# Expert inputs sorted through a buffer in DRAM instead of gathered by one-hot products, in a two-block transformer kernel

## The chip, the cores and the metric

One core of one Trainium2 chip runs the whole program, with all arithmetic in float32. The metric is the device time of one execution in microseconds (us). The kernel before takes 2696.76 us, the median of three runs (2690.66 to 2697.54).

The engines go by their names in the profile: PE multiplies matrices (PEld loads its weights), DVE, ACT and POOL work on vectors, SP only issues DMAs. PSUM (`ps`) is the memory that PE writes. Sixteen DMA engines serve all queues; queue 1 is SP's, queue 10 ACT's, queue 0 POOL's.

## What is computed

Three layers of mixer and experts follow each other over 512 tokens of width 1024. The mixers are a state-space scan beside forgetting attention, a differential attention, and an RWKV-7 time mix. After each one comes a layer norm, a hierarchical mixture of experts, and another layer norm. Only the experts matter here:

```python
def _hier_moe(h, rg_w, rg_b, re_w, re_b, w_gate, w_up, w_down):
    ...
    e_val, e_idx = lax.top_k(jax.nn.softmax(e_logits, axis=-1), TOP_K)     # TOP_K = 2
    ...
    combine = jnp.sum(jax.nn.one_hot(expert_id, N_EXPERTS) * weights[..., None], axis=1)
    for e in range(N_EXPERTS):
        act = jax.nn.silu(hf @ w_gate[e]) * (hf @ w_up[e])                 # hidden width 512
        out = out + combine[:, e:e + 1] * (act @ w_down[e])
```

The first expert layer has 16 experts and the other two have 32. A token goes to two experts, so each layer has 1024 rows of expert input.

## The kernel before

Each token's two rows get a **slot**: the rows of an expert stand together, padded to blocks of `BLK` = 32. `project_and_experts` (L1072) does the output projection, the first norm, the routing and the experts of a layer. A layer has as many blocks as its experts fill: 42, 52 and 52 with this input (146 in all), at least one per expert, and some experts have up to five. The number of blocks is known only on the chip, so every engine runs a loop with a bound read from `table`.

**Inputs of a block.** PE computes them as a product: `gather(n)` (L1254) multiplies a one-hot matrix (which token sits in which of the 32 slots of block n) with all tokens `x_tok`, 16 matmuls into `ps[:, 5]`. DVE makes the one-hot matrix by three small operations (`hot`, L1388), and transposes the result out of PSUM into `xg` (`take_inputs`, L1476), the stationary operand of the gate and up products. `xg` has one buffer. The gather of block g+1 stands in PE's program between the gate/up products of block g and its down product.

**A block on PE** (L1276 to L1294): wait for `xg`; gate and up products, first half, which need the expert's first weight piece; second half, which needs the second piece; the gather of the next block; then the down product, which needs the third piece, and in two halves the transposed hidden values `hT`. ACT applies silu to each half (L1342), DVE multiplies by the up values (L1490) and transposes (L1493) into `hT`.

**Weights.** An expert has three pieces of 2 MB (gate/up half 0, gate/up half 1, down). Three experts are held at a time: two in `ring`, the third in `arena` and `xt_mem`. SP's `follow` (L1161) waits until the last block of expert e has used a piece and then loads the same piece of expert e+3 into its place, in fixed order. Within a queue the loads come one after another.

**Outputs.** DVE copies a block's result into `y_sb` (L1501, two buffers), and ACT stores it to the DRAM buffer `xybuf` by four DMAs of 32 KB (L1325), rows of 1 KB. At the end of the layer POOL gathers each token's two rows from `xybuf` with 8 indirect DMAs (L230). `xybuf` is filled with zeros once, in the first mixer (L482).

**POOL** is otherwise idle during the expert loop. Ahead of it, it loads the gains and offsets of the second norm (L291, L292, and L296, L297).

## Time and profile before

| | us |
|---|---|
| median of three runs | 2696.76 |
| lowest, highest | 2690.66, 2697.54 |
| the profiled execution | 2697.32 |
| its span in the trace | 2695.6 |
| expert loop of the first layer (42 blocks) | 380.7 to 687.4 |
| expert loop of the second layer (52 blocks) | 1063.2 to 1550.7 |
| expert loop of the third layer (52 blocks) | 2190.5 to 2652.0 |

PE is busy for 2343.1 us (87% of the span), DVE for 1000.8 us, ACT for 571.8 us and POOL for 194.1 us. The DMA queues move 616 MB, 575 MB of it on SP's queue.

The profile is of one execution. The busy share of an engine over the whole span says little here, because the three loops have different limits; each has to be read by itself, from the busy share of PE beside that of the DMA engines. A loop's limit may also change inside it, since one expert has one block and the next has five. In rows of the timeline the first column is the start, the second the length, both in us; "[x <-y]" is idle time of the engine ahead of that row and what ended it.

### The profile page before, as it was taken

Reading aid. Unit: us, or ns where it says so; the run is one execution under the profiler, and the core shown is the slowest. Engines: PE = TensorE matmul, PEld = TensorE weight load, DVE = VectorE, ACT = ScalarE, POOL = GpSimd, SP = SyncE. Lnnn points to the kernel's source line nnn. Section 1 sums busy time; section 2 is a strip of 40 time slices with the busy share of each in tenths; the row PEclk is TensorE's granted clock in tenths of the full one; section 3 lists DMA queues with packets and bytes.
Section 4 is the critical chain, followed back from the end, with each engine's and each line's share of the span. In section 5 each row is a group of like instructions: output and inputs, shape, how many; then the busy total and the mean of one; then the engine's idle time right before and its main releaser. Section 6 shows DMA issues by size and latency. Waiting matters only on the chain. (4 is left out here: it accounts for less than half of the span.)

```text
span 2695.6 us, 88071 instructions
## 1 busy us (share of the span) xinstructions
PE 2343.1 (87%) x38568; PEld 1597.3 (59%) x38569; DVE 1000.8 (37%) x2690; ACT 571.8 (21%) x1231; POOL 194.1 (7%) x309
## 2 busy tenths in 40 slices
PE   8997999999999888999757779978889988788972
PEld 4445557777544655777545533458777466566761
DVE  1206353333400854333212254037765443222324
ACT  2035211111300641111101031033433111111111
POOL 1001200000100010000000010012332200000001
PEclk9998999999999999999989889989999999999996
DMA  9202158977421006969999942000001289999995
GB/s 342 112 32 94 49 216 343 409 309 284 164 94 63 32 19 237 403 271 427 429 429 428 426 173 102 0 24 3 3 5 40 106 313 427 429 429 428 413 428 214
DMA packets 83423, 616.42 MB, mean 229 GB/s; under 512 B 19909, under 2 KB 40649, under 8 KB 49242
## 3 DMA queue, kind: packets, MB, share of 16 engines
q1 hardware_dynamic: 45664, 574.98, 51.6%
q10 hardware_dynamic: 31402, 20.06, 2.4%
q0 software_dynamic: 6224, 19.43, 2.3%
q8 instruction: 105, 1.72, 0.3%
q14 instruction: 28, 0.23, 0.0%
HBM read 582.92 MB, written 31.49 MB: 228 GB/s over the span
## 5 line engine op out<-in xcount | busy, mean ns | idle before, releaser
L1282 PE MATMUL ps<-ring,arena 128*32 128x128 f32 x13184 | 411.3, 285 | 104.4 <-DMA ring<-in_experts 71.4
L1282 PEld LDWEIGHTS ps<-ring,arena 128*32 128x32 f32 x13184 | 382.0, 115 | 146.1 <-DMA ring<-in_experts 68.3
L1259 PE MATMUL ps<-x_tok,arena 128*32 128x256 f32 x4768 | 292.2, 384 | 11.0 <-DVE arena L1397 8.3
L1342 ACT ACTIVATE arena<-ps 128x64 f32<-128x64 f32 x292 | 65.5, 224 | 1085.0 <-PE ps L1282 1085.0
L1490 DVE TENSOR_TENSOR arena<-arena,ps 128x64 f32<-128x64 f32 x292 | 64.8, 222 | 615.6 <-ACT arena L1342 615.6
L1282 PE MATMUL ps<-arena 128*32 128x128 f32 x5504 | 171.6, 283 | 48.2 <-DMA arena<-in_experts 39.4
L1259 PEld LDWEIGHTS ps<-x_tok,arena 128*32 128x32 f32 x4768 | 159.8, 112 | 89.4 <-issue 18.9
L1292 PE MATMUL ps<-ring,arena 128*32 128x256 f32 x3296 | 198.2, 379 | 13.0 <-DMA ring<-in_experts 12.9
L1282 PEld LDWEIGHTS ps<-arena 128*32 128x32 f32 x5504 | 158.3, 113 | 67.0 <-DMA arena<-in_experts 45.4
L1232 PE MATMUL ps<-ring,arena 128*128 128x512 f32 x384 | 171.9, 604 | 3.4 <-PEq L2465 1.7
L1292 PEld LDWEIGHTS ps<-ring,arena 128*32 128x32 f32 x3296 | 109.1, 110 | 85.7 <-DMA ring<-in_experts 21.2
L549 PE MATMUL ps<-xt_mem,ring 128*128 128x512 f32 x320 | 137.9, 593 | 0.0
L1232 PEld LDWEIGHTS ps<-ring,arena 128*128 128x128 f32 x384 | 73.0, 194 | 89.8 <-issue 89.5
L1477 DVE STREAM_TRANSPOSE arena<-ps 128x256 f32<-128x256 f32 x149 | 67.1, 450 | 149.2 <-PE ps L1259 149.2
L1779 PE MATMUL ps<-arena,ring 128*128 128x512 f32 x256 | 110.1, 592 | 0.0
L1602 PE MATMUL ps<-xt_mem,ring 128*128 128x512 f32 x256 | 110.0, 592 | 0.0
L549 PEld LDWEIGHTS ps<-xt_mem,ring 128*128 128x128 f32 x320 | 60.6, 190 | 76.5 <-issue 76.4
L1334 ACT ACT_TABLE_LOAD x73 | 93.7, 1283 | 33.1 <-DVE arena L1468 26.4
L1501 DVE COPY arena<-ps 128x256 f32<-128x256 f32 x146 | 62.0, 425 | 94.7 <-PE ps L1292 94.7
L1292 PE MATMUL ps<-xt_mem,arena 128*32 128x256 f32 x1376 | 83.3, 380 | 5.8 <-DMA xt_mem<-in_experts 4.9
L1779 PEld LDWEIGHTS ps<-arena,ring 128*128 128x128 f32 x256 | 48.6, 190 | 61.6 <-issue 61.6
L1602 PEld LDWEIGHTS ps<-xt_mem,ring 128*128 128x128 f32 x256 | 48.6, 190 | 61.2 <-issue 61.2
(449 smaller groups left out, 2938.3 us busy)
## 6 DMA issues: line engine op xcount, KB each, us to landing
ring<-in_experts SPq DMA_DIRECT2D x165, 2048.0 KB, 21.3
arena<-in_experts SPq DMA_DIRECT2D x50, 2048.0 KB, 24.8
xt_mem<-in_experts SPq DMA_DIRECT2D x25, 2048.0 KB, 29.5
ring<-in_mixer_chunks SPq DMA_DIRECT2D x24, 2048.0 KB, 12.8
xybuf<-arena ACTq DMA_DIRECT2D x608, 32.0 KB, 6.8
xybuf<-arena SPq DMA_DIRECT2D x1, 9216.0 KB, 50.9
ring<-gate_rows SPq DMA_DIRECT2D x2, 2048.0 KB, 7.4
rows<-in_ln_g POOLq DMA_DIRECT2D x6, 512.0 KB, 7.5
```

The costliest lines, as they stand in the source:

```text
L549: ins = pe.matmul(bank, w[:, k, j * P:(j + 1) * P], xT[:, k, :], start=(k == 0), stop=(k == NK - 1))
L1232: ins = pe.matmul(ps[:, 2 * j + c, :], mT[:, k, j * P:(j + 1) * P], w[:, k, :], start=(k == 0), stop=(k == NK - 1))
L1259: ins = pe.matmul(ps[to, 5, 0:W], one_hot[:, j, :], x_tok[:, j, q * W:(q + 1) * W], start=(j == 0), stop=(j == NT - 1))
L1282: ins = pe.matmul(ps[at, 2 + half, 0:P], xg[:, k, :], w_gu[half][:, k, q, :], start=(k == 0), stop=(k == NK - 1))
L1292: ins = pe.matmul(ps[at, 4, 0:W], hT[:, f, :], w_d[:, f, q * W:(q + 1) * W], start=(f == 0), stop=(f == NT - 1))
L1334: act.preload_act_table(ACT.Silu)
L1342: act.activation(silu_g[:, half, :], ps[:, 2 + half, 0:HALF], ACT.Silu).then_inc(s_silu[half], 1)
L1477: dve.transpose(xg.rearrange("p k s -> p (k s)"), ps[:, 5, 0:W]).then_inc(s_xg, 1)
L1490: dve.tensor_tensor(hidden[:, half, :], silu_g[:, half, :], ps[:, 2 + half, HALF:P], ALU.mult)\
L1501: dve.tensor_copy(y_sb[:, b, :], ps[:, 4, 0:W]).then_inc(s_y, 1)
L1602: ins = pe.matmul(ps[:, n % 8, :], lhs, rhs, start=(k == 0), stop=(k == NK - 1))
L1779: ins = pe.matmul(bank, w[:, k, j * P:(j + 1) * P], xm[:, k, :], start=(k == 0), stop=(k == NK - 1))
```

## The change

All three expert layers get their block inputs another way, from the third block on.

- A second DRAM buffer, `xbuf`, has the layout of `xybuf`. SP fills it with zeros in the first mixer, after the stream of weights has been issued and ahead of the stores of `gate_rows`. ACT waits for both fills ahead of its first `v` eviction.
- As soon as the slots are known (a new signal, `slotted`, sent by DVE from the operation that writes `slots_i`), POOL writes every token's row (4 KB) to its two slots in `xbuf`, by 8 indirect DMAs of 128 rows. They stand ahead of the loads of the second norm's gains.
- When these 8 have landed, POOL loads block 2 into `x_in` by four DMAs of 32 rows by 1 KB. In its loop it waits until block g+1 has been taken into `xg` and loads block g+3. `x_in` has two buffers.
- DVE's `take_inputs` in the loop transposes from `x_in` and not from PSUM, and `hot` has gone from the loop.
- Blocks 0 and 1 are still gathered by PE. The gather of block 1 now stands ahead of the loop; DVE copies it into `x_in`.
- POOL ends with a wait for its last loads, which nobody uses.

```diff
@@ in the first mixer, SP and ACT
                     stream_mixer(sp, first + SLOTS, first + 8)
+                    sp.dma_start(xbuf.rearrange("(r p) d -> p r d", p=P),
+                                 zeros.unsqueeze(1).to_broadcast([P, xbuf.shape[0] // P, D])).then_inc(zeroed.sem, 16)
                     sp.wait_ge(dve_b.sem, g0 + 1)
...
-                            act.wait_ge(zeroed.sem, 16)
+                            act.wait_ge(zeroed.sem, 32)
@@ project_and_experts, POOL
+                    def load_inputs(start, b):
+                        for q, to in enumerate(quarters):
+                            pool.dma_start(x_in[to, b, :], xbuf[bass.ds(start, BLK), q * W:(q + 1) * W]).then_inc(s_loaded[b], 16)
+
+                    if sent:
+                        load_inputs(SPARE_BLOCK * BLK, 1)
                     pool.wait_ge(*at_step("placed", LAST_TILE_SCALED))
+                    if sent:
+                        pool.wait_ge(*at_step("slotted", 1))
+                        for j in range(NT):
+                            for n in range(2):
+                                pool.indirect_dma_start(out=xbuf, out_offset=bass.IndirectOffsetOnAxis(ap=slots_i[:, n, j:j + 1], axis=0),
+                                                        in_=x_tok[:, j, :], in_offset=None).then_inc(steps["inputs_sent"].sem, 16)
                     load_norm_rows(pool, g_src_2, b_src_2)
...
+                    if sent:
+                        pool.wait_ge(*at_step("placed", TABLED))
+                        fours = value(pool, slice(E + 2, E + 3), high=MAXB // AHEAD)
+                        pool.wait_ge(*at_step("inputs_sent", 2 * NT * 16))
+                        load_inputs(3 * BLK, 0)
+                        with pool.Fori(0, fours) as p:
+                            for b in range(AHEAD):
+                                g = AHEAD * p + b
+                                pool.wait_ge(s_xg, g + 2)
+                                load_inputs((g + 4) * BLK, (b + 1) % AHEAD)
+                        for b in range(AHEAD):
+                            pool.wait_ge(s_loaded[b], fours * 64 + 64)
@@ PE
-                            gather(g + 1)
+                            if not sent:
+                                gather(g + 1)
...
                     pe.wait_ge(*at_step("placed", TABLED))
+                    if sent:
+                        pe.wait_ge(s_xg, 1)
+                        gather(1)
@@ DVE
-                    dve.tensor_copy(ahead_by, slots)
-                    link(dve.tensor_scalar(slots_i, slots, float(BLK), None, ALU.add))
+                    dve.tensor_scalar(slots_i, slots, float(BLK), None, ALU.add).then_inc(steps["slotted"].sem, 1)
+                    link(dve.tensor_copy(ahead_by, slots))
...
                     hot(1, 2)
+                    if sent:
+                        dve.wait_ge(s_loaded[1], 64)
+                        dve.wait_ge(s_gathered, 2)
+                        link(dve.tensor_copy(x_in[:, 1, :], ps[:, 5, 0:W]))
...
                             dve.wait_ge(s_gu[1], g + 1)
-                            dve.wait_ge(s_gathered, g + 2)
-                            take_inputs()
-                            hot(2, 2 * g + 4)
+                            if sent:
+                                after_b = (b + 1) % AHEAD
+                                dve.wait_ge(s_loaded[after_b], p * 64 + 64)
+                                take_inputs(x_in[:, after_b, :])
+                            else:
+                                dve.wait_ge(s_gathered, g + 2)
+                                take_inputs()
+                                hot(2, 2 * g + 4)
```

The order of instructions, at three places. PE, the loop over the blocks of a first or second expert (`ps<-ring,arena` at x64 are the gate and up products, `x_tok,arena` the gather, the last MATMUL row the down product), before:

```order
L1276 UNCONDITIONAL_BRANCH
L1276 ISA
L1279 ISA
L1282 MATMUL ps<-ring,arena 32x128 x64
L1256 REGISTER_ALU
L1259 MATMUL ps<-x_tok,arena 32x256 x16
L1292 MATMUL ps<-ring,arena 32x256 x16
L1276 REGISTER_ALU
L1276 COMPARE_AND_BRANCH
```

and in the changed kernel:

```order
L1309 UNCONDITIONAL_BRANCH
L1309 ISA
L1312 ISA
L1315 MATMUL ps<-ring,arena 32x128 x64
L1326 MATMUL ps<-ring,arena 32x256 x16
L1309 REGISTER_ALU
L1309 COMPARE_AND_BRANCH
```

The 16 gather matmuls between the two products are gone; nothing stands in their place.

DVE, the end of the first block of a pair in the loop (the transposition of the second half of `hT`, then `take_inputs`, `hot`, and the copy of the result), before:

```order
L1493 STREAM_TRANSPOSE arena<-arena 128x64
L1496 REGISTER_ALU
L1477 STREAM_TRANSPOSE arena<-ps 128x256
L1391 TENSOR_SCALAR arena<-arena 128x8
L1392 REGISTER_ALU
L1393 TENSOR_TENSOR arena<-arena,cst 128x256
L1396 REGISTER_ALU
L1397 TENSOR_TENSOR arena<-arena 128x128
L1500 ISA
L1501 COPY arena<-ps 128x256
```

and in the changed kernel:

```order
L1531 TENSOR_TENSOR arena<-arena,ps 128x64
L1533 REGISTER_ALU
L1534 STREAM_TRANSPOSE arena<-arena 128x64
L1539 ISA
L1514 STREAM_TRANSPOSE arena<-arena 128x256
L1547 COPY arena<-ps 128x256
```

The transposition into `xg` now reads `x_in` (in `arena`) and stands directly ahead of the copy of the result.

POOL, from the last fill ahead of the routing (`y_sb`) to the end of its part in the first expert layer, before:

```order
L1190 MEMSET arena 128x512
L291 DMA rows<-in_ln_g 128x1024
L292 DMA rows<-in_ln_b 128x1024
L296 DMA small<-in_ln_g 128x8x1
L297 DMA small<-in_ln_b 128x8x1
L1146 UNCONDITIONAL_BRANCH
```

and in the changed kernel, up to the first load of a block:

```order
L1198 MEMSET arena 128x512
L1202 DMA arena<-xbuf 32x256 x4
L1211 DMA xbuf<-x_tok,arena 2304x1024 x8
L292 DMA rows<-in_ln_g 128x1024
L293 DMA rows<-in_ln_b 128x1024
L297 DMA small<-in_ln_g 128x8x1
L298 DMA small<-in_ln_b 128x8x1
L1152 TENSOR_LOAD arena
L1152 ISA x2
L1202 DMA arena<-xbuf 32x256 x4
```

The eight writes to `xbuf` stand ahead of the four loads of the second norm, and those stand ahead of the load of block 2.

## Rows read from the trace of the kernel before

**Rows 1.** Busy time by window: an engine's us and instructions, PEclk, DMA share, GB/s

```profile
core 0: us, PE busy (x) PEld busy (x) DVE busy (x) ACT busy (x) POOL busy (x), PEclk, DMA share, GB/s
380.00:688.00 308.00, 295.50 (x8068) 236.77 (x8064) 109.69 (x382) 44.49 (x104) 0.00 (x0) 1.00 0.77 310
...
1127.00:1167.00 40.00, 39.54 (x1084) 31.71 (x1080) 14.88 (x52) 5.95 (x13) 0.00 (x0) 1.00 0.52 203
1167.00:1540.00 373.00, 290.15 (x7177) 222.26 (x7172) 96.03 (x335) 41.19 (x94) 0.00 (x0) 0.93 1.00 419
...
2190.00:2652.00 462.00, 391.14 (x9984) 301.91 (x9984) 135.02 (x471) 55.38 (x129) 0.00 (x0) 0.95 0.98 413
```

**Rows 2.** Timeline (start, length) of one block in the first layer, inside an expert

```profile
387.65 3.68 PE L1282 MATMUL ps<-ring,arena 128*32 128x128 f32 x128
...
391.15 1.92 PE L1259 MATMUL ps<-x_tok,arena 128*32 128x256 f32 x32
391.40 0.22 ACT L1342 ACTIVATE arena<-ps 128x64 f32<-128x64 f32 x1 [1.52 <-PE ps L1282]
...
391.91 0.25 DVE L1493 STREAM_TRANSPOSE arena<-arena 128x64 f32<-128x64 f32 x1
...
392.87 1.92 PE L1292 MATMUL ps<-ring,arena 128*32 128x256 f32 x32
393.12 0.45 DVE L1477 STREAM_TRANSPOSE arena<-ps 128x256 f32<-128x256 f32 x1 [0.97 <-PE ps L1259]
...
394.60 3.68 PE L1282 MATMUL ps<-ring,arena 128*32 128x128 f32 x128
```

**Rows 3.** Timeline of DVE and POOL around the slots, first layer, and an indirect DMA

```profile
371.88 0.55 POOL L291 DMA_DIRECT2D rows<-in_ln_g  x1 [12.75 <-DVE x_tok L1375]
...
375.48 0.16 DVE L1461 TENSOR_SCALAR arena<-arena 128x8 uint32<-128x8 f32 x1
...
693.56 0.97 POOL L230 DMA_INDIRECT ring<-xybuf,arena  x1 [0.30 <-issue]
```

**Rows 4.** DMA queues, 52 to 68 us (the zero fill alone): packets, MB, share

```profile
q1 hardware_dynamic: 1648, 6.75, 102.4%
```

**Rows 5.** DMA queues, 1057 to 1065 us (norm rows beside expert weights)

```profile
q1 hardware_dynamic: 181, 2.69, 80.3%
q0 software_dynamic: 116, 0.47, 14.6%
```

**Rows 6.** DMA queues, 1345 to 1435 us (six blocks), and the stores' median landing

```profile
q1 hardware_dynamic: 2596, 37.82, 98.3%
q10 hardware_dynamic: 1152, 0.79, 2.7%
xybuf<-arena ACTq DMA_DIRECT2D x24, 32.0 KB, 6.3
```

**Rows 7.** Timeline of DVE, result copies: a change of expert; four one-block experts

```profile
439.89 0.42 DVE L1501 COPY arena<-ps 128x256 f32<-128x256 f32 x1 [0.44 <-PE ps L1292]
448.12 0.43 DVE L1501 COPY arena<-ps 128x256 f32<-128x256 f32 x1 [0.53 <-PE ps L1292]
...
1376.84 0.42 DVE L1501 COPY arena<-ps 128x256 f32<-128x256 f32 x1 [0.53 <-PE ps L1292]
...
1436.66 0.42 DVE L1501 COPY arena<-ps 128x256 f32<-128x256 f32 x1 [1.93 <-PE ps L1292]
```

**Rows 8.** Timeline of SP: weight loads of layers two and three (start; time over all)

```profile
1167.32 2.07 SPq L1157 DMA_DIRECT2D arena<-in_experts  x2
...
2200.43 20.10 SPq L175 DMA_DIRECT2D ring<-in_experts  x6
```

**Rows 9.** Timeline of the first mixer: stores of the gates, evictions of v

```profile
80.31 0.69 SPq L487 DMA_DIRECT2D gate_rows<-rows  x2
107.47 27.75 SPq L491 DMA_DIRECT2D ring<-gate_rows  x2
...
162.93 2.05 ACT L577 ACTIVATE arena<-ps 128x512 f32<-128x512 f32 x4
```

14 lines of the change are left out of this document (10 added, 4 removed).

## The prediction

> **What bounds the kernel now.** I read the windows by stage first, since the change touches only the three expert loops. In the first (380 to 688 [rows 1]) PE is busy for 295.5 of 308 us at a clock of 1.00 and the DMA engines for 0.77: PE sets the pace. In the second the DMA share is 1.00 from 1167 to 1540, at 419 GB/s, after a dip to 0.52 between 1127 and 1167. In the third it is 0.98 over the whole loop, at 413 GB/s. There the weights set the pace. A block has 192 recorded matmuls (128 gate/up, 32 gather, 32 down), so x8068 is 42 blocks and x9984 is 52.
>
> Then one block in the timeline [rows 2]: gate/up start at 387.65, gather at 391.15, down at 392.87, the next gate/up at 394.60. That is 3.50, 1.72 and 1.73, a period of 6.95 us with no gap. The spacing of DVE's result copies shows where an expert ends: 448.12 - 439.89 is 8.23 [rows 7], 1.3 more than inside; that is the largest kind, and 0.8 is the mean that I use.
>
> Last, the pace where weights are short: four experts of one block each take 1436.66 - 1376.84 = 59.8 us [rows 7], 14.96 each. SP's loads show when a buffer came free: at 1167.32, when the one expert with five blocks (the layer's blocks 9 to 13, counted from 0) had used its first piece, the DMA engines got work again, and they stayed full to the loop's end [rows 1, 8].
>
> **Part 1: PE without the gather.** It removes 1.72 us a block. The gather also covers the wait for `hT`. The second silu starts at 391.40, and the transposition after it at 391.91 for 0.25, so its half of `hT` is there at 392.16 [rows 2]. PE, at the down product from 391.15, does the first half of it until 392.02, and starts the second at about 392.3 (0.1 from DVE to PE, my estimate). It ends at 393.16. The period becomes 5.51: 1.44 saved, 0.28 given back. DVE's 0.45 us for `xg` comes at 392.16, done 392.61, still hidden, and the three operations of `hot` are off DVE. If a further wait came in, it would cost its full length: nothing covers PE any more.
>
> **Part 2: the start of a layer.** The gather of block 1 now stands ahead of block 0 with its one-hot matrix: 1.7 + 0.9 = 2.6 us later. Block 2 needs the whole chain through DRAM. The slots are ready at 375.6, in the first layer [rows 3]. POOL's eight indirect writes take about 0.97 + 0.30 each (the row [rows 3] is of a gather of the same size), to 386. They are 1024 rows of 4 KB, 64 for each DMA engine. Alone, 4 KB packets run at 1648 in 16 us [rows 4], 0.155 us for one on an engine, 10 us in all. Beside weights they are slower: between 1057 and 1065 queue 0 moved 0.47 MB of the norm's rows, 115 of 4 KB, and queue 1 moved 2.69 MB, 164 pieces of 16 KB, in 80.3% of the time [rows 5]. Queue 0 had nothing in the first part of that window, so I read it as one row for one piece, in turns: 0.61 + 0.16 = 0.77 us a row.
>
> First layer: some weights are still under way at the start, so I give the writes until 394. The register load, four issues (0.55 each [rows 3]) and a landing put block 2 at 399. Block 1 ends at 380.7 + 2.6 + 11.0 = 394: 5 us.
> Second layer: the first two experts have one block each, so from 1068 to 1078 six loads are queued, 48 pieces for an engine, against the 64 rows. The rows are through at about 1095; the norm's rows, 16 an engine, stand ahead of the inputs in the same queue (12 us at 0.77), so block 2 starts at 1109.
> Third layer: queue 1 is dry for about 7 us ahead of the next load at 2200.43 [rows 8]; the rows use that hole, and block 2 starts at about 2219, where the two blocks of the first expert end at 2204.
>
> **Part 3: traffic.** A block now loads 128 KB in 1 KB rows. The stores of that shape take 2.7% of 90 us for six blocks [rows 6], 0.40 us a block on all engines. I take 0.40 for the loads too. The scatter is 10 us a layer. Where DMA is full, both lengthen the loop in full. The bound below: 37.82 MB are 18.0 pieces of 2 MB in 98.3% of 90 us, 4.9 each and 14.7 an expert, and the whole period is 14.96 with its store, so 0.26. The bound above is half again as much, 0.6, if reads of such rows cost more than the stores.
>
> **Part 4: nothing.** The second zero fill is as long as the first (9.4 MB at 103 packets a us, 22 us) and stands from 80 to 103. The gate stores queue behind it, but SP's next step is at 107.47 and the last of its two loads at 134.87 is the one awaited; ACT reaches `v` at 162.93 [rows 9]. I cost it at 0: the gates have 27 us to spare and `v` 59; without them each microsecond would count in full. POOL's last unused loads end the layer perhaps 0.3 us later each, 1 in all.
>
> **The sum.** First layer: 42 x 1.44 = -60.5, start +2.6, block 2 +5. Then weights: an expert of two blocks needs 3 x 4.9 + 2 x 0.8 = 16.3 us of DMA and 11.8 of PE. Six of the 16 are such, 27 us short in all; the three buffers absorb most, and walking the blocks leaves +6 (0 to 27). Together -47.
> Second layer: what matters is when DMA is full for good. From 1109, eleven blocks to the last of the five-block expert are 60.6, three changes of expert 2.4, half a gate/up 1.75: 1174, against 1167.3, +7. After that 39 blocks at 0.40, +16. Together +23.
> Third layer: 52 x 0.40 = 21; of the scatter 3, as 7 fit into the hole; and a new hole of 8. The first two experts have two blocks each, and six loads are issued between 2200.43 and 2220.53 [rows 8]. Three of them now come 11 us later, behind block 2 (13 later, one block 1.4 shorter), while only one expert (15 us) is queued. Together +32.
> The three give +8, with the tails +9. The profiled execution took 2697.3, 0.6 over the median: 2706.
>
> **A rule weighed.** In [rows 5] a 4 KB row and a 16 KB piece take turns. The Trainium skill, "DMA: Bandwidth & Descriptors", section "Queues, rings and completion order", has an engine change queues only after a whole packet, typically 9 to 17 descriptors. By that rule the scattered rows would pass in groups and not one by one, which is rival B; for plain norm rows this case's trace speaks against it, and for indirect writes no row here can.
>
> **Rival B, rows in groups (0.20).** If four or more rows pass in one turn (0.31 us each beside weights in place of 0.77), the second layer's writes are through at about 1084 and not 1095. Block 2 comes 11 us earlier, DMA is full for good sooner by as much, and the third layer gains 2: 2693, no change.
>
> **Rival F, faster, the other side (0.18).** The loads slip between weight pieces. At 0.26 in place of 0.40 the 91 full-DMA blocks give back 13 and the first layer's +6 goes: 2687. With B's effect as well it is 2674. It decides at a load price of about 0.3. For it speaks the period of 14.96 [rows 7], against it the stores' share of 2.7% [rows 6].
>
> **Rival S, POOL too slow (0.14).** POOL must issue four loads a block. At 0.55 each that is 2.2, and 6.3 to land as the stores do [rows 6] makes 8.5 against two periods, 11.0. At the indirect 1.27 [rows 3] it is 5.1, and 11.4 in all: just late. Above 1.38 an issue POOL sets the pace. At 1.6, 6.4 a block, the first layer gains 40 x 0.9 = 36 less and its weight waits (+6) vanish, +30: 2736.
> The same page, section "Anatomy of one DMA — SWDGE (gpsimd) path", gives such a DMA 2.0 us fixed plus its bytes; four in series would be 8.3 us a block by that estimate, worse than S, but in this case's trace a block's four stores, 6.3 us each to land [rows 6], fit into periods of 6.95 with room, so they overlap.
>
> **Chances.** The forecast, within 2694 to 2722, has 0.48. The range 2676 to 2738 leaves out B and F combined, and a worse S. What can be told from no change is 0.3%, 8 us: below 2688.7, F nearly whole and a little of B, 0.22; within, most of B and the lower third of the forecast, 0.32; above 2704.9, the rest and S, 0.46.
>
> **What would show it.** First loop: period 5.5, PE gap of 0.3 ahead of the second half of the down product, length near 260 us. Second and third: block 2 waits for `x_in` until about 1109 and 2219, then DMA share 1.0 with queue 0 at 2 to 3% of it, periods of one-block experts 15.3 to 15.4. It is wrong if DVE waits for `x_in` inside the loop (S), if block 2 of layer two starts before 1100 (B), or if one-block experts stay below 15.25 (F). A lower PE clock in the first loop would also break the sum.

## The result, and the profile after

Median of the kernel before 2693.7 us, of the changed kernel 2784.2 (2775.0 to 2785.8): 3.2% slower, ratio 1.032 (95% interval 1.031 to 1.034). The forecast was 2706, with a range up to 2738. The profiled execution of the changed kernel took 2775.0 us, its span is 2773.3; before, 2697.3.

A stage is read here from the row in which VectorE writes the slots (L1461 before, L1497 after) to the first gather of results by GpSimd (L230, L231), because both rows exist in every kernel of this case. The last y copy splits off the tail.

| us | layer one | layer two | layer three |
|---|---|---|---|
| before, slots to gather | 316.7 | 499.0 | 470.4 |
| after | 312.9 | 541.3 | 514.9 |
| difference | -3.8 | +42.3 | +44.5 |
| of it the tail (last y copy to gather) | 4.8 to 8.6: +3.8 | 7.8 to 17.6: +9.9 | 4.8 to 9.9: +5.1 |
| difference without the tail | -7.5 | +32.4 | +39.4 |
| forecast | -47 | +23 | +32 |

All else, the mixers with the second zero fill, came out 5 us shorter. The forecast missed the profiled execution by 69 us, and 39.5 of them, the largest part, are in layer one. The median lies another 9 us above the profiled execution; no view shows where these 9 us went.

The windows of the changed kernel (columns as in [rows 1]):

```profile
core 0: us, PE busy (x) PEld busy (x) DVE busy (x) ACT busy (x) POOL busy (x), PEclk, DMA share, GB/s
380.00:684.00 304.00, 240.02 (x6752) 189.34 (x6744) 71.46 (x253) 44.72 (x105) 93.19 (x181) 0.97 0.89 346
1063.00:1100.00 37.00, 11.95 (x320) 9.11 (x319) 2.62 (x10) 2.18 (x5) 9.12 (x15) 0.75 1.02 393
1100.00:1175.00 75.00, 63.73 (x1769) 51.23 (x1773) 18.87 (x67) 11.35 (x27) 22.08 (x45) 0.94 0.85 323
1175.00:1580.00 405.00, 268.56 (x6240) 203.75 (x6231) 66.13 (x235) 41.88 (x97) 79.00 (x159) 0.83 1.01 410
2228.00:2726.00 498.00, 340.08 (x8328) 255.94 (x8320) 88.05 (x313) 55.40 (x129) 108.64 (x217) 0.87 1.00 402
```

In layer one PE is no longer the bound: 240 us busy of 304, where [rows 1] had 295.5 of 308. DMA isn't full either, 0.89. Something else sets the pace. In the two later layers DMA is full, as before, but moves 402 to 410 GB/s of everything where it moved 413 to 419 of almost only weights. PE's granted clock there is 0.83 to 0.87 in place of 0.93 to 0.95, with more idle time on it; what that costs was not tried apart, and transfers set the pace there.

What ends VectorE's waits in layer one (groups by line: busy us, mean ns, idle us ahead and what ended it):

```profile
L1531 DVE TENSOR_TENSOR arena<-arena,ps 128x64 f32<-128x64 f32 x84 | 18.6, 221 | 103.9 <-ACT arena L1379 103.9
L1547 DVE COPY arena<-ps 128x256 f32<-128x256 f32 x42 | 17.8, 424 | 112.8 <-DMA xybuf<-arena 97.8 <-PE ps L1326 15.0
L1514 DVE STREAM_TRANSPOSE arena<-arena 128x256 f32<-128x256 f32 x42 | 17.0, 405 | 6.8 <-DMA arena<-xbuf 6.8
```

The new wait is not for the loads (L1514, 6.8 us, all at the start). It is in front of the copy of a block's result into `y_sb`: 97.8 us for the **stores** of the block two earlier, which leave the same buffer. The kernel before had no such wait. Single copies on the timeline (start, length, idle ahead):

```profile
421.71 0.42 DVE L1547 COPY arena<-ps 128x256 f32<-128x256 f32 x1 [0.86 <-PE ps L1326]
427.15 0.42 DVE L1547 COPY arena<-ps 128x256 f32<-128x256 f32 x1 [0.87 <-PE ps L1326]
...
448.76 0.42 DVE L1547 COPY arena<-ps 128x256 f32<-128x256 f32 x1 [3.29 <-DMA xybuf<-arena]
456.64 0.42 DVE L1547 COPY arena<-ps 128x256 f32<-128x256 f32 x1 [4.37 <-DMA xybuf<-arena]
463.97 0.42 DVE L1547 COPY arena<-ps 128x256 f32<-128x256 f32 x1 [3.81 <-DMA xybuf<-arena]
```

427.15 - 421.71 is the period that Part 1 forecast: 5.44 (forecast 5.51). It holds where the stores are on time. Then it becomes 7.3 to 7.9, longer than the 6.95 with the gather [rows 2].

Why the stores are late is seen in the DMA queues between 440 and 540 us (packets, MB, share of 16 engines). First the kernel before, then the changed one:

```profile
q1 hardware_dynamic: 2560, 37.23, 88.9%
q10 hardware_dynamic: 2678, 1.82, 5.7%
```

```profile
q1 hardware_dynamic: 2545, 37.00, 90.9%
q10 hardware_dynamic: 2544, 1.74, 5.5%
q0 software_dynamic: 1750, 1.80, 5.2%
```

Queue 1 brings weights in 16 KB packets, queue 10 carries the stores. A block's stores are 192 packets (1152 for six blocks [rows 6]), 12 on each engine: eight of 1 KB and four that end the four DMAs. In the changed kernel the two queues passed 2545 and 2544 packets: one for one. At 2544 in 100 us a block's stores take 192 / 25.44 = 7.55 us, and that is the period measured. Queue 10 fills 5.5% of the engines' time and is still saturated: each of its small packets waits its turn beside a large one (the experiments below test this). In the kernel before it already passed as many (2678), but PE's period of 6.95 us asked for no more, and VectorE never waited for a store. Two numbers of [rows 6] misled: the share of 2.7% and a landing of 6.3 us, neither of which shows how many turns are left.

Last, the starts and the tails. Block 2's first product in each layer, and GpSimd's first load of a block in layer two, issued when the eight writes have landed; then the end of layer one (the last y copy, the first gather) after and before:

```profile
399.73 1.50 PE L1315 MATMUL ps<-ring,arena 128*32 128x128 f32 x24 [4.63 <-DVE arena L1514]
1082.56 4.36 POOL L1202 DMA_DIRECT2D arena<-xbuf  x8 [13.86 <-DMA xbuf<-x_tok,arena]
1103.46 1.94 PE L1315 MATMUL ps<-arena 128*32 128x128 f32 x32 [25.68 <-DVE arena L1514]
2248.53 1.72 PE L1315 MATMUL ps<-ring,arena 128*32 128x128 f32 x28 [8.58 <-DVE arena L1514]
679.13 0.43 DVE L1547 COPY arena<-ps 128x256 f32<-128x256 f32 x1 [0.87 <-PE ps L1326]
687.70 1.03 POOL L231 DMA_INDIRECT ring<-xybuf,arena  x1 [6.56 <-POOLq L1154]
```

```profile
687.38 0.42 DVE L1501 COPY arena<-ps 128x256 f32<-128x256 f32 x1 [0.44 <-PE ps L1292]
692.19 1.07 POOL L230 DMA_INDIRECT ring<-xybuf,arena  x1 [317.43 <-POOLq L1146]
```

### The profile page after: what moved, and what is told of

Read it like the earlier page. It is cut to its first block and busy times, and to the rows that moved or that the text cites. A ratio compares the mean times of both kernels' runs of the same rounds, so it can differ in the third digit from the quotient of the medians.

```text
span 2773.3 us, 80244 instructions
## 1 busy us (share of the span) xinstructions
PE 2184.5 (79%) x33992; PEld 1459.6 (53%) x33993; DVE 871.4 (31%) x2255; ACT 571.6 (21%) x1231; POOL 520.5 (19%) x941
## 5 line engine op out<-in xcount | busy, mean ns | idle before, releaser
L1315 PE MATMUL ps<-ring,arena 128*32 128x128 f32 x13184 | 434.4, 294 | 158.4 <-DMA ring<-in_experts 103.9
L1315 PEld LDWEIGHTS ps<-ring,arena 128*32 128x32 f32 x13184 | 397.8, 119 | 212.2 <-DMA ring<-in_experts 109.4
L1202 POOL DMA_DIRECT2D arena<-xbuf x608 | 302.9, 499 | 1000.5 <-DVE arena L1514 900.8
L1326 PE MATMUL ps<-ring,arena 128*32 128x256 f32 x3296 | 235.5, 419 | 105.1 <-DMA ring<-in_experts 58.2
L1379 ACT ACTIVATE arena<-ps 128x64 f32<-128x64 f32 x292 | 65.5, 224 | 1152.6 <-PE ps L1315 877.7
L1315 PE MATMUL ps<-arena 128*32 128x128 f32 x5504 | 180.1, 292 | 78.2 <-DMA arena<-in_experts 40.3
L1315 PEld LDWEIGHTS ps<-arena 128*32 128x32 f32 x5504 | 166.2, 118 | 99.4 <-DMA arena<-in_experts 47.9
L1326 PEld LDWEIGHTS ps<-ring,arena 128*32 128x32 f32 x3296 | 103.8, 117 | 203.2 <-issue 72.7
L1326 PE MATMUL ps<-xt_mem,arena 128*32 128x256 f32 x1376 | 96.4, 413 | 46.5 <-DMA xt_mem<-in_experts 23.6
L1326 PEld LDWEIGHTS ps<-xt_mem,arena 128*32 128x32 f32 x1376 | 42.6, 116 | 87.2 <-issue 33.2
L1825 PEld LDWEIGHTS ps<-arena,ring 128*128 128x128 f32 x256 | 48.6, 190 | 61.6 <-issue 61.6
L1648 PEld LDWEIGHTS ps<-xt_mem,ring 128*128 128x128 f32 x256 | 48.6, 190 | 61.2 <-issue 61.2
L1534 DVE STREAM_TRANSPOSE arena<-arena 128x64 f32<-128x64 f32 x292 | 71.8, 246 | 10.0
```

The source lines that it names most:

```text
L1202: pool.dma_start(x_in[to, b, :], xbuf[bass.ds(start, BLK), q * W:(q + 1) * W]).then_inc(s_loaded[b], 16)
L1315: ins = pe.matmul(ps[at, 2 + half, 0:P], xg[:, k, :], w_gu[half][:, k, q, :], start=(k == 0), stop=(k == NK - 1))
L1326: ins = pe.matmul(ps[at, 4, 0:W], hT[:, f, :], w_d[:, f, q * W:(q + 1) * W], start=(f == 0), stop=(f == NT - 1))
L1379: act.activation(silu_g[:, half, :], ps[:, 2 + half, 0:HALF], ACT.Silu).then_inc(s_silu[half], 1)
L1534: dve.transpose(hT[:, 2 * half:2 * half + 2, :].rearrange("p f s -> p (f s)"), hidden[:, half, :])\
L1648: ins = pe.matmul(ps[:, n % 8, :], lhs, rhs, start=(k == 0), stop=(k == NK - 1))
```

## The experiments

Five questions: what the stores, the loads, the scatter and the tail cost, each by itself; whether the stores' wait is a landing time or a rate; what sets the rate; and whether a kernel faster than both follows. Kernels with stale inputs hand other rows to the layers behind layer one. These still have 52 blocks in layer two, perhaps on other experts, but 48 or 50 instead of 52 in layer three. So I read such kernels by layer one, by layer two with care, and not by their totals.

| kernel | median us | ratio to before | layer one | two | three (blocks) | layer-one waits for stores |
|---|---|---|---|---|---|---|
| before | 2693.7 | 1 | 316.7 | 499.0 | 470.4 (52) | none |
| after | 2784.2 | 1.032 | 312.9 | 541.3 | 514.9 (52) | 97.8 |
| before, no gather | 2629.3 | 0.975 | 277.1 | 485.8 | 458.3 (48) | 65.5 |
| after, no loads in the loop | 2685.7 | 0.996 | 285.7 | 509.9 | 475.3 (50) | 64.7 |
| after, no scatter | 2747.1 | 1.019 | 302.0 | 524.7 | 505.7 (50) | 89.7 |
| after, tail fixed | 2766.1 | 1.025 | 312.1 | 537.0 | 508.8 (52) | 101.9 |
| after, no stores in the loop | 2736.5 | 1.017 | 283.8 | 533.8 | 505.5 (48) | none |
| after, four y buffers | 2779.5 | 1.032 | 316.7 (44) | 543.6 | 519.9 (52) | 73.1 |
| after, stores first | 2783.2 | 1.033 | 314.1 | 547.1 | 513.7 (52) | 80.8 |
| no loads, stores by GpSimd | 2694.5 | 1.000 | 280.5 | 517.7 | 486.2 (50) | 10.4 |
| layer one alone, tail fixed | 2686.5 | 0.997 | 308.4 | 498.0 | 470.8 (52) | 95.2 |
| the same, stores split | 2681.5 | 0.995 | 302.0 | 497.8 | 471.0 (52) | 48.2 |
| before plus the loads | 2745.9 | 1.019 | 316.5 | 519.4 | 498.4 (52) | none |
| layer one alone, weights in 8 KB | 2670.4 | 0.991 | 287.3 | 504.5 | 475.1 (52) | none |
| before, weights in 8 KB | 2703.8 | 1.004 | 315.4 | 504.8 | 475.9 (52) | none |
| layer one alone, its weights in 8 KB | 2664.7 | 0.989 | 284.1 | 497.8 | 470.9 (52) | 6.4 |

The last column is the idle time of VectorE ahead of the y copy that the stores ended, in us, between 380 and 692. Layer one with four y buffers works 44 blocks in place of 42.

**Before, without the gather.** In the loop:

```diff
-                            gather(g + 1)
-                            dve.wait_ge(s_gathered, g + 2)
                             take_inputs()
-                            hot(2, 2 * g + 4)
```

> The kernel before with the loop's one-hot gather left out on PE, and the one-hot and its wait left out on VectorE; nothing is put in their place, so all blocks work on the inputs of the first two, which leaves out the gathering of inputs. No extra transfer exists. Theory S (the stores of y on queue 10 can't keep up with a shorter period, whatever queue 0 does): waits of the y copy for the stores appear here too, layer one's blocks stay at 6.3 to 7 us, layer one gains 10 to 30 us of its 316.7, total 2660 to 2685. Rival Q (the stores are late only because queue 0's packets share the engines): no such wait, period 5.5, layer one gains 50 to 60, total 2630 to 2645. Layers two and three gain little under both (0 to 10 each), since weights bound them.

The wait is there with no queue 0 at all:

```profile
L1498 DVE COPY arena<-ps 128x256 f32<-128x256 f32 x42 | 17.8, 424 | 84.9 <-DMA xybuf<-arena 65.5 <-PE ps L1291 19.4
```

Layer one is 39.6 us shorter, more than theory S gave (10 to 30) and less than Q (50 to 60), the total at Q's lower edge through layer three's fewer blocks. S is right about the mechanism: a shorter period alone makes the stores late. The loads make it worse: between 440 and 540 us this kernel passes 2774 packets on queue 1 and 2868 on queue 10, the changed one 2545 and 2544. With a third busy queue a turn comes round later, and a block's 192 packets need 7.55 us in place of 6.69.

**After, without the loads in the loop, and without the scatter.**

```diff
-                        with pool.Fori(0, fours) as p:
-                            for b in range(AHEAD):
-                                g = AHEAD * p + b
-                                pool.wait_ge(s_xg, g + 2)
-                                load_inputs((g + 4) * BLK, (b + 1) % AHEAD)
...
-                                dve.wait_ge(s_loaded[after_b], p * 64 + 64)
+                                dve.wait_ge(s_loaded[after_b], 64)
```

> The changed kernel with the loads of x rows in the loop left out (the scatter stays, blocks from the third on work on stale inputs). Theory S: layer one's stage keeps its store waits and stays at 290 to 305 us (312.9 in the changed kernel, of which the last loads' tail is about 4). Rival Q: it falls to 255 to 270. Layers two and three: if a block's loads cost 0.8 us of the transfers, 52 blocks each of which about 32 are bound by weights give back 20 to 30 each, beside tails of 10 and 5; if they cost 0.4, 12 to 15 beside the tails. Total 2700 to 2730 for the first, 2735 to 2750 for the second, under theory S.

Layer one fell by 27.2 us to 285.7 with 64.7 us of store waits left, as S said, though S had 290 to 305. Queue 10 passed 2846 packets beside 2807, much as without the gather. Layer two fell by 31.4; 8 of them are its tail (17.6 to 9.6). The total was lower than I expected, in part by layer three's two blocks less.

```diff
-                        for j in range(NT):
-                            for n in range(2):
-                                pool.indirect_dma_start(out=xbuf, out_offset=bass.IndirectOffsetOnAxis(ap=slots_i[:, n, j:j + 1], axis=0),
-                                                        in_=x_tok[:, j, :], in_offset=None).then_inc(steps["inputs_sent"].sem, 16)
...
-                        pool.wait_ge(*at_step("inputs_sent", 2 * NT * 16))
```

> The changed kernel with the eight scatters and the wait for them left out (the loads read zeros from DRAM, so the inputs from the third block on are left out). Theory: the start through DRAM costs what block 2's first product shows (it came 24 to 29 us after the slots were known); without the scatter it comes 10 to 15 us earlier, and each layer gains 8 to 14 us, total 2742 to 2760. Rival: where weights bound the stage the early start is given back for want of weights, total over 2770, the gain then in layer one alone.

10.9 less in layer one, within the 8 to 14 expected, and 16.6 in layer two, a little more. An early start isn't given back where weights bound the stage, as far as layer two's other routing lets this be said.

**After, with the tail fixed.**

```diff
-                        with pool.Fori(0, fours) as p:
+                        with pool.Fori(0, fours - 1) as p:
...
-                            pool.wait_ge(s_loaded[b], fours * 64 + 64)
+                            pool.wait_ge(s_loaded[b], fours * 64)
```

> The changed kernel with the last turn of GpSimd's loop of loads left out: two blocks' rows that no block uses aren't loaded, and the wait at the end needs them no longer. Computes all of it. Theory: the stage's end falls from 8.6, 17.7 and 9.9 us after the last y copy to about 5 to 8 each, total 2765 to 2770. Rival: the end waits for the last stores of y, or for the draining of the queue, just as long, total within 3 us of 2784.

The tails became 4.8, 9.6 and 4.8, together 17 us shorter, and the median fell by 18; the three tails had added 18.8. In the profiled execution layer one took back nearly all of it ahead of the last copy (312.1), so single stages are known to some 3 us.

**After, without the stores in the loop.**

```diff
-                                store_quarters(g * BLK, freed, (2 * half, 2 * half + 1))
...
-                            dve.wait_ge(s_stored[b], p * 64 + 64)
+                            dve.wait_ge(s_stored[b], 64)
```

> The changed kernel with the stores of y in the loop left out, and so their waits (nearly all of the experts' results stay out of DRAM, the final gather reads what is there). Theory S (the stores are what holds the blocks of layer one): its median block falls to 5.5, and its stage to 255 to 265 us (312.9 in the changed kernel, 285.7 without the loads). Rival L (the loads themselves hold the blocks, by their traffic or their own waits): the stage stays over 280. Layers two and three each lose 15 to 30 us, as their transfers shrink by 128 small packets per block.

The median block is 5.44 us, so the stores are what holds the blocks. But the stage is 283.8, not 255 to 265; that is the length which rival L gave, though with its median block L's reason can't be the right one. Layers two and three lost less than thought. Something else is missing from the forecast, too (below).

**Landing time or rate.** With two buffers, a late landing and a slow queue look alike. Four buffers help against the first only; so does an earlier issue.

```diff
+            AHEAD = 4 if l == 0 else 2
-                x_in = take(AHEAD, D // 4)
+                x_in = take(X_AHEAD, D // 4)
```

> The changed kernel with four buffers for y in layer one in place of two (layers two and three keep two; layer one works two blocks of padding more, 44 in place of 42). Computes all of it. This splits theory S. S-latency (the queue could carry a block's stores in 5.5 us, but a store lands 8 to 12 us after its issue, and two buffers allow one in flight): the waits for stores vanish, median block 5.5 to 6, layer one 270 to 285, total about 2750. S-rate (queue 10 carries one block in 6.5 to 7.2 us beside the weights and the loads, whatever is buffered): the waits stay, median block near 7, layer one 312 to 325 with its two blocks more, total 2780 to 2795.

```diff
+                            store_quarters(g * BLK, freed, range(4))
                             for half in range(2):
-                                store_quarters(g * BLK, freed, (2 * half, 2 * half + 1))
```

> The changed kernel with all four stores of a block's y issued ahead of the first silu, where two stood ahead of each silu. Computes all of it. S-latency: the last two land about 1.5 to 2 us sooner, a period of two blocks shrinks by that, minus 0.5 to 0.8 us per block of layer one, total 2745 to 2765. S-rate: nothing is gained (2775 to 2790); the first silu is later by two issues of about 0.05 to 0.1 us, hardly seen.

Neither moved the time. (One expectation puts an issue by ScalarE at 0.05 to 0.1 us; in the traces two take 0.80. Layer one was 1.2 us longer with all stores first, within its noise.) With four buffers, from 440 to 540 us, queues (packets, MB, share) and the stores' median us from issue to landing:

```profile
q1 hardware_dynamic: 2512, 36.70, 90.3%
...
q10 hardware_dynamic: 2511, 1.72, 5.4%
...
xybuf<-arena ACTq DMA_DIRECT2D x60, 32.0 KB, 23.1
```

The backlog grew until a store took 23.1 us to land, at the same 2511 packets in 100 us, again equal to the weights' 2512. It is a rate. The median block went from 7.3 to 7.0 only, and the stage, with two blocks more, was 3.8 us longer.

**The same rows through queue 0.** Without the loads in the loop; the four stores of a block are issued by GpSimd:

```diff
-                                store_quarters(g * BLK, freed, (2 * half, 2 * half + 1))
+                                pool.wait_ge(s_y, g + 1)
+                                store_y(g * BLK, (b - 1) % AHEAD)
```

> The changed kernel without the loads of x rows in the loop (inputs stale, left out as before) and with the stores of y issued by GpSimd on queue 0 in place of ScalarE on queue 10; to be read against the kernel without the loads (2686, layer one 285.7). The loads' trace shows that queue 0 moves such rows as 2048-byte packets, 4 to an engine and block, where queue 10 has 8 of 1024. S-rate with turns by the packet: half the turns, the store waits of layer one vanish, stage 265 to 272, total 2655 to 2670. S-latency: four issues of 0.5 each and a longer way add 2 to 4 us to the landing, the waits grow, stage 295 to 310, total over 2700.

```profile
L1549 DVE COPY arena<-ps 128x256 f32<-128x256 f32 x42 | 17.8, 424 | 52.6 <-PE ps L1337 42.2 <-DMA xybuf<-arena 10.4
...
q1 hardware_dynamic: 2791, 40.65, 95.0%
q0 software_dynamic: 2091, 2.14, 6.1%
```

Queue 0 packs the rows in twos, 8 turns a block in place of 12, and isn't at queue 1's count: the waits fell from 64.7 to 10.4 us (9.07 of them ahead of the very first copy) and the median block from 6.66 to 5.54. The stage gained 5.2 only, since the first stores stood behind the scatter (first y copy 23.9 us after the slots instead of 15.1) and the tail grew to 10.6. Layers two and three got 7.8 and 10.9 us longer, so the total went the wrong way, while the waits of layer one did what S-rate expected. Why the later layers lost was not looked into beyond their tails (17.3 and 12.7 in place of 9.6 and 4.8), which are most of it.

**Layer one alone, and with the stores split.**

```diff
-            sent = True
+            sent = l == 0
```

> The change in layer one alone, with the last turn of the loop of loads left out (the tail's fix); layers two and three as before the change. Computes all of it. From the stage lengths: layer one 312.9 less the tail's 3.8 stands against 316.7, so a gain of 7 to 8 us, total 2684 to 2690. Rival: the runs with the tail's fix gave layer one 312.1, so the last y copy moved later by what the tail gave back; then the gain is 3 to 5, total 2689 to 2693.

```diff
+                                pool.wait_ge(s_y, g + 2)
+                                store_two((g + 1) * BLK, b)
```

> The kernel of the run before (layer one alone, tail fixed) with the last two quarters of each y stored by GpSimd on queue 0 instead of ScalarE on queue 10, in layer one. Computes all of it. S-rate (a queue's packets each wait their turn beside a 16 KB packet of weights): queue 10 has 4 packets per engine and block instead of 8, queue 0 has 6 of 2048 bytes instead of 4; at 0.65 to 0.8 us a turn both fit in 5.5 us, the waits for stores all but vanish, median block 5.5 to 5.9, layer one 285 to 297, total 2662 to 2676. Rival: six issues of 0.5 us on GpSimd and its waits in turn make it the late one, layer one 300 to 315, total over 2680.

The first came out 0.3% shorter than the kernel before (interval 0.996 to 0.998), its layer one 8.3 us. The split gave 6.4 us of layer one and not 11 to 23, and its lengths are those of the rival, which blames GpSimd's six issues. But GpSimd isn't the late one: it waits 111.5 us for VectorE ahead of its loads. The queues, 440 to 540:

```profile
q1 hardware_dynamic: 2533, 37.01, 91.0%
q0 software_dynamic: 2593, 2.65, 7.7%
q10 hardware_dynamic: 1252, 0.86, 2.7%
```

Queue 10 is relieved and now queue 0 is the saturated one, 2593 against 2533. I had counted six turns on queue 0 and left out the packets that end each DMA; with them it is 12, as queue 10 had.

**Before plus the loads.** The loads alone (and the second zero fill); no computing engine waits for them.

```diff
+                        with pool.Fori(0, fours - 1) as p:
+                            for b in range(AHEAD):
+                                g = AHEAD * p + b
+                                pool.wait_ge(s_xg, g + 2)
+                                pool.wait_ge(s_loaded[(b + 1) % AHEAD], p * 64 + 64)
+                                load_inputs((g + 4) * BLK, (b + 1) % AHEAD)
```

> The kernel before, to which only the loads of x rows are added in all three layers, as the changed kernel issues them (less the last two blocks'), into a buffer that nothing reads; no scatter, the gather stays on PE, nobody waits for the loads but the stage's end. Computes all of it, from the right inputs, so the blocks are 42, 52 and 52. It sizes the loads by themselves. If a block's loads take 0.8 us from the weights where these bound the stage: layers two and three 18 to 28 us longer each, layer one 3 to 10 (its queue 10 has 7.0 us a block), total 2735 to 2755. If 0.4, as the prediction had it: 8 to 14 each, layer one 0 to 3, total 2712 to 2725.

Layer one is unmoved (-0.2), layers two and three got 20.4 and 28.0 us longer. In layer three that is 0.56 us for each of the 50 blocks loaded. In layer two the DMA engines are full only from 1167 on [rows 1], and the loads ahead of that cost nothing: the five-block expert's first piece comes free 107.9 us after the slots in both kernels. So the 20.4 us belong to the 39 blocks that Part 3 counted, 0.52 each. So both layers show some 0.5 to 0.6 where Part 3 had 0.40.

**One DMA per block.** If the packets that end a DMA take turns too, fewer DMAs should help.

```diff
-                        for q in two:
-                            act.dma_start(xybuf[bass.ds(start, BLK), q * W:(q + 1) * W], y_sb[quarters[q], b, :])
+                        act.dma_start(xybuf[bass.ds(start, BLK), :].rearrange("s (q w) -> q s w", q=4), y_sb[:, b, :])
```

The stores of both halves now go out ahead of the first silu.

> Layer one alone with the tail fixed, and the stores of a block's y by one DMA of 128 rows of 1 KB in place of four of 32, in all layers. Computes all of it. If every packet of a queue takes a turn, the 4-byte one that ends a DMA too, queue 10 needs 9 turns a block in place of 12: at 1.6 turns per us 5.6 us, waits for stores nearly gone, median block 5.5 to 5.9, layer one 283 to 293 (308.4), total 2660 to 2672 (2686.5). If only data packets take turns, or the bytes count: nothing moves, layer one 303 to 309, total 2680 to 2690.

```diff
-                        for q, to in enumerate(quarters):
-                            pool.dma_start(x_in[to, b, :], xbuf[bass.ds(start, BLK), q * W:(q + 1) * W]).then_inc(s_loaded[b], 16)
+                        pool.dma_start(x_in[:, b, :], xbuf[bass.ds(start, BLK), :].rearrange("s (q w) -> q s w", q=4)).then_inc(s_loaded[b], 16)
```

> As the run before, and a block's x rows are loaded by one DMA in place of four too (layer one): queue 0 needs 5 turns a block in place of 8. Computes all of it. Turns: queue 0 wasn't the late one, so little is added, layer one 0 to 6 shorter than in the run before, total 2656 to 2670. Rival: one long DMA lands later than four short ones, or GpSimd takes longer to issue 128 rows at once than four times 32, so waits for loads appear: layer one 295 or more.

> The change in all three layers with the tail fixed (2766), with one DMA per block for stores and one for loads. Computes all of it. Layer one as in the run before, about 20 to 28 us shorter. Layers two and three: where weights bound them, the data packets' time stays and 6 turns of 4 bytes at 0.009 go, so little; where stores held a row of short blocks, some comes back: 3 to 15 each. Total 2715 to 2742. If only data packets take turns: total 2755 to 2767.

> The kernel before with one DMA per block for the stores of y. Computes all of it. PE sets its period of 6.95 in layer one and weights set the two others, and there was no wait for a store, so no gain is expected from turns: total 2688 to 2697. Rival: with fewer turns on queue 10 the weights come sooner (their rate in layer one was 1.60 turns per us, as high as queue 10's), which would show as 3 to 10 us less, 2680 to 2690.

All four were far slower: 2944.9, 2950.6, 3073.0 and 2917.9 us, their layer one 367.1, 386.8, 384.6 and 354.6. (The 0.009 us for a 4-byte packet in the third expectation is too long: queue 10's share of the time with and without most of its short packets, 5.7% for 2678 packets before and 4.2% for 1389 here, puts one at some 0.003 to 0.006 us.) The test failed for a reason of its own, which the first one's queues (440 to 540) and its y copies show:

```profile
q10 hardware_dynamic: 1389, 1.38, 4.2%
...
481.76 0.42 DVE L1546 COPY arena<-ps 128x256 f32<-128x256 f32 x1 [0.87 <-PE ps L1326]
502.57 0.42 DVE L1546 COPY arena<-ps 128x256 f32<-128x256 f32 x1 [16.23 <-DMA xybuf<-arena]
```

1.38 MB are some 1350 packets of 1 KB, which leaves some 40 that end a DMA, for ten DMAs: four each, where a DMA on 16 engines has 16. So a block's 128 rows went over 4 engines, 32 on each, and at about 0.63 us a turn that is 20 us, the wait of the row. The Trainium skill, "DMA: Bandwidth & Descriptors", section "Why a DMA increments its semaphore by 16 and not by 1", lets the slowest dimension set how many engines a DMA uses; here it was the four quarters, and the trace agrees. These runs say nothing about the short packets' turns, but the 32 turns on an engine are a second sight of the same price.

**Weights in 8 KB packets.** The other side of the turn, with the stores as they were; beside it the control.

```diff
+        def load_halves(eng, to, src, sem):
+            for h in range(2):
+                of = slice(h * NK * CH // 2, (h + 1) * NK * CH // 2)
+                eng.dma_start(to[:, of], src(of)).then_inc(sem, 16)
...
-            eng.dma_start(slot(n % SLOTS), expert_src(l, e, kind)).then_inc(arrived[n % SLOTS].sem, 16)
+            load_halves(eng, slot(n % SLOTS), expert_src(l, e, kind), arrived[n % SLOTS].sem)
```

> Layer one alone with the tail fixed (2686.5), and every chunk of weights, the mixers' too, loaded by two DMAs of 8 KB rows in place of one of 16 KB rows. Computes all of it. If a store's packet waits one turn of a weight packet: a turn on an engine falls from 0.63 to about 0.36 us, queue 10's 12 turns from 7.5 to 4.3 us a block, the waits for stores go, the median block of layer one falls to 5.5 and its stage from 308.4 to 280 to 290, total 2658 to 2670. If the stores' queue has a pace of its own (each packet's write or its semaphore): the waits stay, layer one 303 to 310, total 2680 to 2690. Rival: 8 KB packets move fewer GB/s, then all layers lose, total over 2700.

> The kernel before with every chunk of weights in 8 KB rows, as control. Computes all of it. 8 KB packets cost nothing by themselves: 2690 to 2700. If they cost 1% of the transfers' rate: about 2715. A gain would need stores or other small transfers to be late in the kernel before, which its trace doesn't show: no wait for them.

On the kernel with the change in layer one the waits for stores vanished, and with them 21.1 us of its stage. Groups of VectorE in layer one; queues and the stores' landing, 440 to 540:

```profile
L1552 DVE COPY arena<-ps 128x256 f32<-128x256 f32 x42 | 17.8, 424 | 50.3 <-PE ps L1331 50.3
...
q1 hardware_dynamic: 4883, 35.56, 89.2%
q10 hardware_dynamic: 2978, 2.04, 6.9%
...
xybuf<-arena ACTq DMA_DIRECT2D x60, 32.0 KB, 5.8
```

Queue 10 now passes 2978 packets against 4883 and is no longer full; the same stores, a block's 128 KB in four DMAs, land in 5.8 us. This is the test that the turn is one packet of weights: nothing on the stores' side was touched, and a pace of the stores' queue by itself would have stayed. The control lost 10.6 us, in layers two and three above all (504.8 and 475.9), where weights bound the time.

**Layer one's weights alone in 8 KB.** The same edit under `if l == 0`.

> Layer one alone with the tail fixed, and only the experts' weights of layer one in 8 KB rows; the mixers' and the other layers' in 16 KB rows as before. Computes all of it. Layer one as with halves everywhere, 285 to 290 us; layers two and three back from 504.5 and 475.1 to 498 and 471, the rest as before: total 2658 to 2665. Rival: the cost of 8 KB packets lies in layer one as well and the others' 11 us were drift: 2668 to 2674.

2664.7 us, ratio 0.989 (interval 0.987 to 0.990): shorter than both kernels. The change that cost 3.2% in all three layers is kept here in layer one only, with the tail fixed and that layer's weights in 8 KB rows. Its copies of y in layer one:

```profile
437.96 0.42 DVE L1568 COPY arena<-ps 128x256 f32<-128x256 f32 x1 [0.87 <-PE ps L1347]
445.10 0.42 DVE L1568 COPY arena<-ps 128x256 f32<-128x256 f32 x1 [0.87 <-PE ps L1347]
450.54 0.42 DVE L1568 COPY arena<-ps 128x256 f32<-128x256 f32 x1 [0.87 <-PE ps L1347]
...
647.07 0.43 DVE L1568 COPY arena<-ps 128x256 f32<-128x256 f32 x1 [2.30 <-DMA xybuf<-arena]
654.69 0.42 DVE L1568 COPY arena<-ps 128x256 f32<-128x256 f32 x1 [4.09 <-DMA xybuf<-arena]
```

5.44 within an expert, and 7.14 where it changes. The last two rows are the 6.4 us of waits in the table, and they repeat the test inside one kernel. From about 636 us queue 1 brings the next mixer's weights, which here come in 16 KB packets again (97 packets with 1.42 MB up to 640 us). Queues from 644 to 648 us:

```profile
q1 hardware_dynamic: 90, 1.33, 87.6%
q0 software_dynamic: 89, 0.09, 7.4%
q10 hardware_dynamic: 90, 0.06, 5.3%
```

All three queues are at one count again, and the waits for stores are back. With the mixers' weights in 8 KB too, in the run before, there was none.

## Why the prediction was wrong, step by step

**Part 1, PE without the gather: right about PE, wrong that PE would set the pace.** The period is 5.44 against 5.51 wherever nothing else waits, and the gap ahead of the second half of the down product is there. The step that failed is to book 42 x 1.44 us with PE's new period as the only bound. The term for the queue that stores the results was put at nothing. The forecast had the stores as 0.40 us of traffic and 6.3 us of landing [rows 6], and never as a queue with a rate of its own. Its sentence that a further wait would cost its full length was right, but it did not ask which wait would be next. Rival S did ask about a queue, but about GpSimd's issues (0.50 us each, four in 2.23 us), which were no bound. In place of 5.51 us the queue of the stores set 7.55 us a block. What it cost: layer one without its tail is 304.4 us after, 282.4 with 8 KB packets, 279.3 with those in layer one alone, so 22 to 25 us.

**The rest of layer one, 14 to 17 us.** Even without waits for stores the stage lies 29.5 to 32.6 us under the kernel before, not 47. One part is that an expert's change costs more when the blocks are shorter. PE's idle time ahead of an expert's first product, for which the trace names no releaser, in layer one before and in the last experiment (us in total, times, longest):

```profile
PE ps L1282 <- issue: 9.4, 15, 1.0
```

```profile
PE ps L1336 <- issue: 17.2, 16, 1.5
```

0.63 us each became 1.08, some 7 us over 15 changes; Part 1 carried the 0.8 us of a change over unchanged. Why a change costs more was not tested. The second part is the weights. The last experiment has two long intervals between copies, 13.65 and 9.28 us where a change of expert otherwise takes 6.6, and PE waits for weights in both. They are some 10 us too long together, where the forecast had 6; the kernel before has no such wait in this loop:

```profile
514.60 3.64 PE L1347 MATMUL ps<-xt_mem,arena 128*32 128x256 f32 x32 [4.00 <-DMA xt_mem<-in_experts]
602.82 1.93 PE L1347 MATMUL ps<-ring,arena 128*32 128x256 f32 x32 [2.71 <-DMA ring<-in_experts]
```

The two late stores at its end cost another 4. The start is a small part: the third block's copy comes 5.6 us later after the slots than before (32.0 against 26.4) in the changed kernel and 4.6 in the last experiment. The forecast's 7.6, less the 1.44 us saved in each of three blocks, is 3.3. With the 0.07 us a block that the period came out shorter, these parts add up to some 14 us in the last experiment.

**Part 2, the start: the right time, in layer two by luck.** Block 2 came at 399.7 (399 by the forecast), 1103.5 (1109), and in layer three 28.9 us after the slots (32.6 by the forecast). Layer two's slots were ready 4.6 us earlier than before, so there 48.6 us after the slots stand against 49.5. But two errors cancel in it. The writes had landed by 1082.56, 27.7 us after the slots, where the forecast had 35.5: queue 1 was nearly dry from 1060 to 1068 us, and 817 of the 1152 packets of queue 0's writes passed in those 8 us. The way from there to block 2 took 20.9 us and not 14. Leaving out the scatter gives 11 and 17 us of layers one and two.

**Part 3, the loads: low in both layers.** 20.4 and 28.0 us measured by themselves, against 16 and 21; a block's loads cost 0.52 and 0.56 us where DMA is full, not 0.40. After the loads and the tail, 12.0 and 11.4 us are left in layers two and three, for which the forecast had a start of 7 and 11. In layer two the first weight piece of the five-block expert came free at 1176.92, 122 us after the slots, against 107.9 before: 14 us later and not 7. The eleven blocks ahead of it took 71.8 us where the forecast had 63, and 11.3 us of waits for stores stand among them. So the two layers missed by 9 and 7 us.

**Part 4, the tails: wrong.** 1 us forecast, 18.8 measured, and 18 came back by the fix. I costed the last unused loads by their time on the engines. What was missing is that GpSimd ends its part with a wait for them: it issues the last four at 678.92 us, and after 6.56 us of idle (the row of 687.70) starts the gather. The landing by itself is only 1.9 us of that; what fills the rest was not tested, but it goes when the loads are left out. The second zero fill did cost nothing: the mixers aren't longer.

**The rivals.** B (rows in groups) would have started block 2 of layer two before 1100: it came at 1103.5. The writes themselves were through nearly as early as B had them (1082.56 against 1084), but by the hole in queue 1, and not in groups. The scattered rows beside weights, 1074 to 1090 us of the changed kernel:

```profile
q1 hardware_dynamic: 367, 5.24, 76.8%
q0 software_dynamic: 369, 1.36, 20.8%
```

367 against 369: one row of 4 KB for one piece of 16 KB, as Part 2 took it. The rule on which B stood (the Trainium skill, "DMA: Bandwidth & Descriptors", section "Queues, rings and completion order": a queue is left only after a packet of typically 9 to 17 descriptors) isn't what these rows show, neither for indirect writes nor for the stores. Equal counts alone would also fit groups of equal length on both queues, but the counts stay equal in 4 us, in which an engine passes only 5 or 6 packets of each queue: 93 and 93 from 1088 to 1092 us, 90, 89 and 90 in the last experiment. F needed loads under 0.3 us, they took 0.52 and 0.56. S is out. The case that came, a slower kernel by a store wait, was none of them.

## What to carry to other kernels

Beside a queue's share of the DMA engines, count its packets per block, the ones that end each DMA included, and compare with the packets of the large stream on the same engines: where the two counts are equal and somebody waits for the small queue, it is full, however few bytes it moves. Ask this ahead of every edit that shortens a period, for the queues of all who must keep up, not only for the new one. And put an exchange of PE work for transfers only where PE sets the pace: here it pays in layer one (0.3% of the whole time as it is, 1.1% with smaller weight packets) and costs 30 to 40 us in each layer that weights bound.

## What the runs showed of the hardware

- Two busy queues pass packets one for one, 16 KB on the one and 1, 2 or 4 KB on the other: 2545 and 2544 in 100 us, 2512 and 2511 with four buffers, 2533 and 2593 for queue 0. The counts agree only with the short packets that end each DMA among them (1.74 MB are 1700 of 1 KB, of 2544). That these take turns is read from the counts; no run changed their number alone.
- Halving the weight packets nearly doubled the turns (4883 for 2545) and cost 0.4% of the whole time where nothing waited for turns.
- A DMA of four groups of 32 rows ran on 4 engines, four DMAs of 32 rows on all 16.
- GpSimd's queue moved rows of 1 KB two to a packet (128 packets a block with the ends, 192 on ScalarE's): 8 turns in place of 12.
